# Two layers of four-branch mixing on one Trainium2 core: four weight remainders per layer computed on GpSimd in place of VectorE

## The reference

```python
h = rmsnorm(x, g_mix[l]) * (1.0 + sc1) + sh1
z = h @ w_in[l]
parts = dict(zip(IN_NAMES, jnp.split(z, IN_OFFSETS, axis=-1)))
y_a = pool_mixer(parts['pool_u'], pool_w[l], pool_scale[l])
y_b = chunk_band_attention(...)                # four heads, relative bias
y_c = dsa_attention(...)                       # keys chosen by an index score, 64 largest
y_d = mla_attention(...)                       # latent keys and values
mix = group_rmsnorm(jnp.concatenate([y_a, y_b, y_c, y_d], axis=-1), g_group[l])
x = x + gt1 * (mix @ w_out[l])
```

## Time and profile before

| | |
|---|---|
| median of 3 runs | 1553.72 us (1553.58 to 1553.84) |
| profiled execution, its own time | 1553.36 us |
| its span in the trace | 1551.6 us |
| TensorE busy | 1528.0 us (98%) |
| VectorE busy | 1293.0 us (83%) |
| ScalarE busy | 909.2 us (59%) |
| GpSimd busy | 256.5 us (17%) |
| granted TensorE clock | 0.999 |

### The profile page before, as it was taken

The page is one execution under the profiler, slowest core; times in us unless marked ns, Lnnn a source line. Parts: engine busy times, 40 slices in busy tenths (PEclk is TensorE's granted clock), DMA queues, the critical chain, the costliest instruction groups (busy, mean ns, idle before and its releaser), DMA issues. The chain is left out here.

```text
span 1551.6 us, 32166 instructions
## 1 busy us (share of the span) xinstructions
PE 1528.0 (98%) x13098; PEld 1508.2 (97%) x13098; DVE 1293.0 (83%) x1999; ACT 909.2 (59%) x1572; POOL 256.5 (17%) x270
## 2 busy tenths in 40 slices
PE   6999999999999999999999999999999999999998
PEld 6999999999999999999999999989999999899998
DVE  7998898997898888888997888899888889985553
ACT  6555458765455545459765455677545466765453
POOL 4322000112210222000112211101221001021100
PEclk9999999999999999999999999999999999999999
DMA  9999974579997899864579998445899963567761
GB/s 371 366 370 325 325 252 163 164 254 324 316 321 265 307 305 324 300 230 164 177 251 331 315 347 278 150 137 165 318 337 346 312 233 123 168 208 236 239 211 42
DMA packets 110612, 402.17 MB, mean 259 GB/s; under 512 B 12403, under 2 KB 12659, under 8 KB 110337
## 3 DMA queue, kind: packets, MB, share of 16 engines
q1 hardware_dynamic: 109136, 395.34, 73.5%
q0 software_dynamic: 1328, 4.78, 0.8%
HBM read 399.02 MB, written 1.05 MB: 258 GB/s over the span
## 5 line engine op out<-in xcount | busy, mean ns | idle before, releaser
L1875 DVE TENSOR_TENSOR WL<-ring,WH 128x1024 fp32r<-128x1024 f32 (+1 forms) x502 | 598.6, 1227 | 151.6 <-ACT WH L1347 151.1
L608 PE MATMUL PS<-HH,WH 128*128 128x256 f32 (+2 forms) x2600 | 617.8, 279 | 1.8 <-DVE WL L1875 1.0
L608 PE MATMUL PS<-HL,WH 128*128 128x256 f32 (+1 forms) x2592 | 602.1, 277 | 0.0
L1347 ACT ACTIVATE WH<-ring 128x1024 fp32r<-128x1024 f32 (+1 forms) x502 | 506.9, 1049 | 48.0 <-PE PS L608 40.9
L608 PEld LDWEIGHTS PS<-HH,WH 128*128 128x128 f32 (+1 forms) x2600 | 488.3, 188 | 4.0 <-issue 2.3
L608 PEld LDWEIGHTS PS<-HL,WH 128*128 128x128 f32 x2592 | 481.2, 188 | 0.5
L608 PE MATMUL PS<-HH,WL 128*128 128x256 f32 (+1 forms) x2592 | 372.0, 277 | 0.3
L1901 DVE CUSTOM_DVE_ANT_0 ring<-ring,CB,VC 128x1024 f32<-128x1024 f32 x240 | 333.5, 1407 | 3.1 <-DMA ring<-in_ada 3.1
L608 PEld LDWEIGHTS PS<-HH,WL 128*128 128x128 f32 x2592 | 332.1, 188 | 1.2 <-DVE WL L1875 1.1
L608 PE MATMUL PS<-AH,WH 128*128 128x256 f32 x1056 | 292.4, 277 | 0.0
L608 PE MATMUL PS<-AH,WL 128*128 128x256 f32 x1056 | 292.0, 277 | 0.0
(11 more groups left out here) (252 smaller groups left out, 1496.7 us busy)
## 6 DMA issues: line engine op xcount, KB each, us to landing
ring<-in_up SPq DMA_DIRECT2D x176, 512.0 KB, 5.8
ring<-in_ada SPq DMA_DIRECT2D x144, 512.0 KB, 6.2
ring<-in_ffn SPq DMA_DIRECT2D x132, 512.0 KB, 5.1
ring<-in_mod SPq DMA_DIRECT2D x96, 512.0 KB, 6.0
ring<-in_down SPq DMA_DIRECT2D x88, 512.0 KB, 5.7
ring<-in_win SPq DMA_DIRECT2D x64, 512.0 KB, 5.5
ring<-in_wout SPq DMA_DIRECT2D x32, 512.0 KB, 4.3
ring<-in_winv SPq DMA_DIRECT2D x8, 512.0 KB, 4.1
```

The costliest lines, as they stand in the source:

```text
L608: return e.matmul(out, lhsT, rhs, start=start, stop=stop, skip_group_check=skip)
L1347: e.activation(half_of(i)[0], slot_of(("half", i, 0))[:, 0:w], ACT.Copy).then_inc(s_hi, 1)
L1875: return e.tensor_tensor(out, a, b, op)
```

## The change

Of each mixer of kind 2, the remainders of four half panels (7, 11, 15 and 19, counted from the mixer's first) are computed by GpSimd in place of VectorE, with the same subtraction on the same tiles. GpSimd counts a semaphore of its own, `s_lop`; the helper `lo_done(i)` tells every place that waits for remainder i (TensorE, and SyncE for the ring slot) which of the two semaphores to wait for and to which count. On GpSimd the first three stand ahead of `wide_pools` and the fourth behind it.

```diff
+POOL_LO = {"ffn": (), "mix1": (), "mix2": (7, 11, 15, 19)}
...
+        pool_halves = [2 * UNIT0[n] + h for n, (kind, _, _) in enumerate(SUBS) for h in POOL_LO[kind]]
+
+        def lo_done(i):
+
+            before = sum(h < i for h in pool_halves)
+            return (s_lop, before + 1) if i in pool_halves else (s_lo, i + 1 - before)
...
                     if was == "half":
-                        e.wait_ge(s_lo, o + 1)
+                        e.wait_ge(*lo_done(o))
...
+            def lo_half(i):
+
+                wh, wl = half_of(i)
+                e.wait_ge(s_hi, i + 1)
+                e.tensor_tensor(wl, slot_of(("half", i, 0))[:, 0:units[i // 2][1]], wh.bitcast(F32), ALU.subtract).then_inc(s_lop, 1)
...
-                    wide_pools(n)
+                    for h in POOL_LO[kind]:
+                        if h == 19:
+                            wide_pools(n)
+                        lo_half(2 * UNIT0[n] + h)
...
-                lo(u0 + 3)
+                lo_half(2 * u0 + 6)
                 lo(u0 + 4)
                 key_turn()
                 index_sum(0)
                 largest(0, (0,))
-                lo(u0 + 5)
+                lo_half(2 * u0 + 10)
...
-                lo(u0 + 7)
+                lo_half(2 * u0 + 14)
                 largest(0, (6,))
...
                 unit_rows(n, o0 + 2)
-                lo_half(2 * u0 + 19)
                 tile_rest(n, o0 + 1)
```

More of the change, by code:

```diff
@@ L145, in build @@
         s_hi, s_lo, s_half = sem("s_hi"), sem("s_lo"), sem("s_half")
+        s_lop = sem("s_lop")
         s_cload, s_cspread, s_cb, s_mod, s_modh = (sem("s_" + k) for k in ("cload", "cspread", "cb", "mod", "modh"))
@@ L621, in cols @@
                 if first:
-                    e.wait_ge(s_lo, i + 1)
+                    e.wait_ge(*lo_done(i))
                     for k in range(KD):
@@ L646, in first_pair @@
                 if k == 0:
-                    e.wait_ge(s_lo, h + 1)
+                    e.wait_ge(*lo_done(h))
                     if h % 2 == 0:
@@ L675, in first_paced @@
                 e.wait_ge(s_hh, k + 1)
-                e.wait_ge(s_lo, 1)
+                e.wait_ge(*lo_done(0))
                 mm(PS[0:4, 4, 0:256], half_of(0)[0][:, 0:4], HH[:, k, 0:S])
@@ L767, in early_pair @@
                 for p in range(2):
-                    e.wait_ge(s_lo, h + p + 1)
+                    e.wait_ge(*lo_done(h + p))
                     for k in range(KD):
```

## The result

The changed kernel takes 1557.45 us (median of 14 runs, 1555.90 to 1558.38), the kernel before 1553.70 beside it (14 runs, 1552.89 to 1554.62): ratio 1.0024, 95% interval 1.0015 to 1.0032. The prediction was 1557.0. The profiled execution took 1557.69 us, with a span of 1555.8 us and a granted clock of 0.997. It enters the first mixer of kind 2 already 1.05 us later than the profile of before, from parts that the change doesn't touch, so I compare times between landmarks inside the mixer and not times from the start. (TensorE's granted clock in that execution was 0.59 from 20 to 25 us and 0.72 from 25 to 30 us, so partly on the lower of its two levels, 1.2 GHz, where the profile of before has 1.00 (TensorE had been busy 8.0 of the first 20 us, 9.3 in the profile of before); whether that makes the whole 1.05 us is not shown.)

A forecast was written before the change was run, and what follows sets the result against it. TensorE, busy 98% of the span, was taken to bound the kernel. New waits of 0.2 + 1.5 us per mixer, 3.3 for two, on the profiled 1553.36 gave 1556.7, plus 0.36 for the median 1557.0; range 1553.5 to 1558.8.

The forecast's parts named there:

- the relief: VectorE, kind-2 mixers: the removed remainders give nothing, as VectorE waits for TensorE or ScalarE; at most 4.4 us.
- the step that I had named: ScalarE's step ending at 1028.71, behind half 19: VectorE would wait there, so removing that half gives 0, at most 1.1 us.
- GpSimd's own time: GpSimd's subtraction of 128 x 1024 takes 2.35 us when it starts freely, with 3.13 as the upper bound.
- Exclusion: VectorE reading two SBUF tiles and GpSimd reading SBUF exclude each other for a whole instruction; 1.7 us per mixer.
- Half 7: GpSimd delays half 6 on VectorE, ending at 973.88, so TensorE waits 0.2 us more for that remainder.
- Half 11: GpSimd gets in among VectorE's seven sums, delaying them 2.05 us; TensorE waits 1.5 us for half 10's remainder.
- Halves 15 and 19: Beside rounds and halves 14 and 18 on VectorE: cost 0, at worst 0.2 us for 15 and 0.1 for 19.
- The sum per mixer: Each kind-2 mixer: 0.2 for half 7 plus 1.5 for half 11, 1.7 us; 3.3 for two with roundings kept.
- VectorE keeps its place: Rival at the seven sums: GpSimd gets in only behind them, TensorE waits 0.9 us; 2.2 us in all, 1555.9; chance 0.10.
- a sharing: Rival: both engines run at half speed, TensorE waits 0.6 us; 1.2 in all, 1554.9; chance 0.12 together with no exclusion.
- longer hold: Rival: GpSimd's own time is 3.13 us, TensorE waits 0.95 and 2.35 us; together 6.6 us, 1560.3; chance 0.10.
- TensorE's delay is carried through: Behind the row maxima VectorE's work starts with TensorE's scores, so the idle 2.21 us moves along and gives nothing back.

The follow-up runs named there:

- The kernel with 8 columns: The changed kernel with GpSimd subtracting only 8 of 1024 columns of each moved half, the rest left out: 1553.81 us against 1553.91 before, ratio 1.0000.
- half 11 behind half 10: The changed kernel, but GpSimd begins the remainder of half 11 only when VectorE has done that of half 10: ratio 1.0010 to the kernel before.
- halves 18 and 19: The kernel before with only the remainders of these two halves moved to GpSimd, behind `wide_pools`: 1552.60 us, ratio 0.9993.
- the doubled operation: The changed kernel with GpSimd making the subtraction of half 11 twice, one behind the other: 1564.52 us, ratio 1.0064 to the kernel before.

## Why the prediction was right

**What bounds the kernel, and the relief.** Both as put. The kernel with 8 columns shows the relief at 0. In the changed kernel VectorE's wait at the row maxima grows from 0.27 to 1.06 us, and behind half 19's old place VectorE waits for ScalarE, 0.66 and 0.35 us. VectorE's timeline after, which answers to the earlier trace rows:

```profile
1006.27 0.69 DVE L2315 TENSOR_REDUCE SMALL<-PS 128x4 f32<-128x512 f32 x1 [1.06 <-PE PS L626]
...
1030.55 0.61 DVE L1896 SCALAR_TENSOR_TENSOR YL<-PS,VC,YH 128x128 fp32r<-128x128 f32 x2 [0.66 <-ACT YH L1505]
...
1031.51 0.35 DVE L1890 TENSOR_SCALAR SQ<-SQ,SMALL 128x256 f32<-128x256 f32 x1 [0.35 <-ACT SMALL L1499]
```

The one detail that differs: VectorE meets ScalarE already at the tile before, 0.66 us at `YH`, ahead of the step that I had named.

**GpSimd's own time.** 2.35 us was taken, between 2.28 and 3.13; measured over the eight operations (count, ns min/median/max, first and last start):

```profile
L548 POOL TENSOR_TENSOR WL<-ring,WH x8: 2373/2396/2427, 971.5 to 1314.0; 128x1024 fp32r<-128x1024 f32 x8
```

So the 3.13 of the nearest row did contain a hold, as argued from the earlier trace rows. The estimate halved from the page of the Trainium skill (GPSIMD Engine Reference, 3.1 Elementwise — side-by-side cycle accounting), 2.25, is 0.15 too low here.

**Exclusion, and what each half costs.** Half 7: 0.2 predicted, 0.22 measured. Half 11: a hold of 2.05 and a wait of 1.5 predicted, 1.97 and 1.46 measured. As forecast, one of the seven sums takes the whole hold and ends just behind GpSimd (count, ns min/median/max, first and last start):

```profile
L1896 DVE SCALAR_TENSOR_TENSOR SCR<-SCR x7: 350/352/2326, 983.0 to 987.3; 128x128 f32<-128x128 f32 x7
```

Halves 15 and 19: 0 predicted; 15 holds half 14 for 0.50 us (1.72 for 1.22), and VectorE's slack ahead of the row maxima covers it, with 1.06 us of waiting left. The sum per mixer: 1.7 predicted, 1.68 and 1.75 in the fronts. "VectorE keeps its place" falls with the 2326 ns inside the sums, "a sharing" with a hold that lasts until GpSimd's end, "longer hold" with 2.40. So in this kernel the engines don't meet at semaphores alone, as the first section has it, but also where both read SBUF.

**That TensorE's delay is carried through.** The back is 57.19 for 57.16: the late waits move with the delay and give nothing back. In TensorE's timeline after, first mixer, the first of them has split in two, and the others stand as they were (in the second mixer the first stays whole, 0.76):

```profile
1029.45 0.41 PE L827 MATMUL PS<-identr,SQ 128*128 128x128 f32 x2 [0.66 <-DVE YL L1896]
1035.59 0.41 PE L827 MATMUL PS<-identr,SQ 128*128 128x128 f32 x2 [0.19 <-DVE YL L1896]
1041.83 1.13 PE L626 MATMUL PS<-SQ,SCR 64*128 64x256 f32 x8 [0.45 <-ACT SCR L1685]
1046.47 1.08 PE L626 MATMUL PS<-SCR 128*128 128x64 f32 x8 [0.66 <-DVE SQ L1893]
1048.15 1.09 PE L1208 MATMUL PS<-identr,SCR 128*128 128x128 f32 x8 [0.38 <-ACT SCR L1685]
```

**What the prediction missed** is not in its sum but in its scope. It looked only at the halves that the change moves, and its rule names only VectorE operations with two SBUF tiles, though the scaling of one SBUF tile was held as well. In two expectations made with the same rule the direction held and the size didn't: half 11 behind half 10 (0.2 expected per mixer, 0.59 measured) and halves 18 and 19 (1.3 to 1.5 us expected for both mixers, 1.15 between the landmarks). Both times the hold fell on a chain that I had passed over. In a third, the doubled operation, the holds came as expected, and the missing 3.1 us were TensorE's clock.

## What to carry to other kernels

Work handed to GpSimd is not free because GpSimd is idle: look for the VectorE instructions that start while it reads SBUF. In these runs those with two SBUF tiles, and a scaling of one, waited until GpSimd's instruction ended; those that read PSUM did not. Follow that delay past the next meeting point that you know of, to every remainder that the bounding engine wants on the way. A long wait of that engine can cost more than its length: in the doubled operation TensorE waited 3.4 us and then worked on at half its clock. Relief on VectorE was worth something only right ahead of a wait of the engine that bounds the kernel; a list of those waits says which instruction to move, and among the halves tried here half 18 was that one. Where the busy time of the relieved engine does not fall by what was taken from it, look for an instruction that is being held.

## What the runs showed of the hardware

- A GpSimd subtraction of 128 x 1024 in float32 with two SBUF inputs took 2.37 to 2.43 us, and 0.20 to 0.28 us for 8 columns; a memset of 128 x 1024 took 0.95 to 0.96 us.
- A GpSimd operation of 2.4 us held VectorE's chain of dependent sums for 1.97 us; the same engine's memsets (2.9 us) held it not at all.
- After a wait of 3.43 us TensorE's granted clock was 0.50 (1.2 GHz) from 992 to 994 us; after waits of 1.37 and 1.40 us it stayed at 1.00 (2.4 GHz).
- VectorE's scaling of one SBUF tile by a column (TENSOR_SCALAR, 128 x 256) was held as well: 0.92 us beside GpSimd's reading, 0.35 without. The Trainium skill lists this operation among those that can take the shared port pair (SBUF — State Buffer, Who interferes with whom), and the trace agrees. MAX8 and MATCH_REPLACE8 of one SBUF tile kept their 0.43 and 0.41 us beside it.
